# A transformer kernel on one core: GpSimd's second unit per layer norm in two halves, and the value products of the compressed stage in another order

## The chip, the core and the metric

The kernel runs on one core of one Trainium2 chip, as one program with one launch. The metric is the device time of that program in microseconds (us). The kernel before takes 1454.27 us, the median of three runs (1453.06 to 1454.77).

The engines have the profile's names: PE is TensorE (matrix products), ACT is ScalarE, DVE is VectorE, POOL is GpSimd, and SP issues most of the DMAs. Each runs its own list of instructions in the order in which the program was written, and they wait for each other through semaphores.

## The reference

Two transformer blocks over 256 tokens of width 1024, in fp32. The first block has a mixer with attention, a cross attention to a memory, and a SwiGLU, each with an RMS norm behind it. The second block has two layers. The part that matters here is the layer norm that closes each of its sublayers, and the shared keys and values that are taken from the state between the two layers:

```
def post_norm(x, sub, g, b):
    return layer_norm(DN_ALPHA * x + sub, g, b)
...
    for layer in range(DEPTH_2):
        if layer == N_A_LAYERS:
            shared = nsa_shared_kv(h, kv_w, cmp_pe, cmp_w1, cmp_b1, cmp_w2)
        h = post_norm(h, 0.5 * swiglu(h, ...), ln_g[layer, 0], ln_b[layer, 0])
        ...
        h = post_norm(h, mix, ln_g[layer, 1], ln_b[layer, 1])
        h = post_norm(h, 0.5 * swiglu(h, ...), ln_g[layer, 2], ln_b[layer, 2])
```

`kv = h @ kv_w` in `nsa_shared_kv` has six slots. Two of them, the values of the selected blocks and of the window, are the products "v2" and "v2w" below.

## The kernel before

**Tiles.** Tokens lie on the 128 partitions in two blocks, tb 0 and tb 1. A weight matrix is read in units of 128 x 2048 fp32 numbers (1 MB) through a ring of three slots. Every product is made in three passes of rounded fp32: ACT casts a unit to its high part `whi`, then DVE or POOL subtracts to get its low part `wlo`, and PE adds high times high, high times low and low times high. The state is split in the same way into `st_hi` (ACT) and `st_lo` (DVE), after PE has transposed it through PSUM. So each unit passes DMA, ACT, DVE or POOL, PE.

**Who makes the low parts.** DVE makes most of them (L2037). `BY_POOL` lists the units that POOL makes (`split`, L2797), among them the first two units behind each of five layer norms: "sgv", ("ffn", 2), "v2", "k2" and ("ffn", 4). ACT's `split` (L1453) casts a unit in one instruction.

**A layer norm.** The text names the norms by the state that they hand on: ln0 (in front of "sgv", at 608 us of the span), ln1 (in front of ffn 2, 753 us), ln2 (in front of "v2", 936 us), and ln4 (in front of ffn 4, 1258 us). A further norm closes the SwiGLU of layer 1's first sublayer (in front of "k2", 1150 us). For each token block DVE adds the branch to the state out of PSUM and takes statistics (`sum_out`, L2115 and L2121), makes mean and variance (L2107, L2108), then makes two passes that centre the halves of the row (`centre`, L2131) and two that scale them and add the offset (`scale`, L2144). These four passes are scalar_tensor_tensor instructions with two tensors from SBUF, and `gb` holds gain and offset. The two scale passes have no wait between them. The reciprocal root between them is POOL's (`var_root`, L2787). PE then transposes the two halves of the block (`turn_st`, L712), ACT copies them to `st_hi` (L1484), and DVE subtracts to get `st_lo` (`st_out`, L2059).

**POOL's order** around such a norm is `layer_norm(n, unit)`: split of the first unit, root of block 0, split of the second unit, root of block 1. ACT casts the second unit as soon as PE has let go of its slot in the ring.

**PE's order** behind a norm is `by_block`: both halves of block 0 are transposed (the first half already ahead of the end of the sublayer before), then come the products of block 0, for each unit and half of the row high times high (L766), weight's low part (L777), row's low part (L785). Behind the last high pass or the last low weight pass of block 0 it transposes the first half of block 1, and the second half a little later. For ln2 the "units" are "v2" and "v2w", of 256 columns each, so a pass of four matmuls is half as long there.

**DVE's order for ln2** differs from that of the other norms: the two `st_out` of block 0 stand between the sums of block 1, ahead of its variance. For ln0 only the first one does, and the second stands behind the variance.

Of the kernel before, what the change touches and what calls it, by code (L numbers as in the profile page):

```python
# [23 lines left out]
F32 = mybir.dt.float32  # L24
F32R = mybir.dt.float32r
I32 = mybir.dt.int32
ALU = mybir.AluOpType
# [3 lines left out]
P = 128  # L31
D = 1024
S = 256
KD = D // P
# [11 lines left out]
RING = 3  # L46
# [31 lines left out]
def build(nc, A, out):  # L78
    ctx = ExitStack()
    with ctx:  # L80
# [3 lines left out]
        def sem(name):  # L84
            return ctx.enter_context(nc.semaphore(name))


        raw = sb("raw", [P, RING, UNIT])
        minus_half = sb("minus_half", [P, 1])
        warm = sb("warm", [P, 16])  # L90
        whi = sb("whi", [P, RING, UNIT], F32R)
        wlo = sb("wlo", [P, RING, UNIT], F32R)
        st_hi = sb("st_hi", [P, 16, S], F32R)
        st_lo = sb("st_lo", [P, 16, S], F32R)
# [5 lines left out]
        res = sb("res", [P, 2, D])  # L100
# [69 lines left out]
        ws = carve(12288, 8, P)  # L170
# [7 lines left out]
        v2 = carve(9216, 2, 2, S)  # L178
# [40 lines left out]
        gain_ready = sem("gain_ready")  # L219
        half_hi_ready = sem("half_hi_ready")  # L220
        half_lo_ready = sem("half_lo_ready")
        whi_ready = sem("whi_ready")
        wlo_ready = sem("wlo_ready")
        w_used = sem("w_used")
        bank_full = [sem(f"bank_full{b}") for b in range(8)]
        bank_read = [sem(f"bank_read{b}") for b in range(8)]
        hi_rounded = sem("hi_rounded")
# [40 lines left out]
        unit_len = []  # L268
        first = {}
# [94 lines left out]
        split_no = {}  # L364
# [141 lines left out]
        def bank(key):  # L506
            return ps[:, use[key][0], :]
# [10 lines left out]
        def read(key, i=0):  # L518

            b, n = use[key]  # L520
            return bank_read[b], n + 1 + i
# [26 lines left out]
        for name in ("sgv", ("ffn", 2), "v2", "k2", ("ffn", 4)):  # L548
            BY_POOL |= {first[name], first[name] + 1}
        BY_POOL |= {first["ffn", n] + 3 for n in range(5)}  # L550

        def half_ready(name, tb, h):

# [108 lines left out]
        def _(pe):  # L662
# [176 lines left out]
            for h in range(2):  # L839
                pe.matmul(gain_rows(h), ones, gb[0:1, 1, 512 * h:512 * h + 512], start=True,  # L840
                          stop=True).then_inc(gain_ready, 1)
# [14 lines left out]
            u = first["kidx"]  # L856
# [340 lines left out]
            for n, j in enumerate(SGU_ORDER):  # L1197
# [7 lines left out]
                for m in MIX_AFTER.get(j, ()):  # L1205
# [4 lines left out]
            swiglu(2, "ln1", res, ahead=lambda: turn_st("ln2", res, 0, 0))  # L1210


            by_block([(first[name], KD, 256, 0, [bank(name)[:, tb * S:tb * S + S] for tb in range(2)], [name, name],
                       True, True) for name in ("v2", "v2w")], st="ln2", src=res)
            def cmp_in(slot):
                key = ("cin", slot)
                room(key)
# [220 lines left out]
        def _(act):  # L1438
# [9 lines left out]
            def split(u, s, q, n=UNIT):  # L1448
                act.wait_ge(raw_loaded[s], 32 * q if s < 2 else 32 * (q + 1))
                if not isinstance(u, int) or u >= RING:  # L1450

                    act.wait_ge(w_used, u - 2)
                act.copy(whi[:, s, 0:n], raw[:, s, 0:n]).then_inc(whi_ready, 1)  # L1453

            def upto(u):
                while nxt[0] <= min(u, UNITS - 1):
# [564 lines left out]
        def _(dve):  # L2021
# [29 lines left out]
            def st_out(name, tb, tiles=KD, k0=0, part=None):  # L2051

                for q in range(tiles // 4):
                    if part not in (None, q):
                        continue
                    key = ("st", name, tb, q)
                    dve.wait_ge(hi_rounded, split_no[key] + 1)
                    hi, lo = (x[:, k0 + 4 * q:k0 + 4 * q + 4, tb * P:tb * P + P] for x in (st_hi, st_lo))
                    dve.tensor_tensor(lo, bank(key).rearrange("p (k t) -> p k t", k=4), hi.bitcast(F32),  # L2059
                                      ALU.subtract).then_inc(*is_read(key))  # L2060
# [49 lines left out]
            def add_out(n, tb, h, halved):  # L2110

                f = 2.0 if halved else 1.0
                key = ("y", n, tb, h)
                dve.wait_ge(*full(key))
                dve.scalar_tensor_tensor(tmp[:, tb, 512 * h:512 * h + 512], res[:, tb, 512 * h:512 * h + 512], f * ALPHA,  # L2115
                                         bank(key), ALU.mult, ALU.add).then_inc(*is_read(key))

            def stats_out(n, tb, h):

                dve.wait_ge(*read(("y", n, tb, h)))  # L2120
                link(dve.bn_stats(stats[:, tb, 6 * h:6 * h + 6], tmp[:, tb, 512 * h:512 * h + 512]))  # L2121

            def sum_out(n, tb, h, halved):

                add_out(n, tb, h, halved)
                stats_out(n, tb, h)
# [7 lines left out]
            def norm_out(n, tb, between=None):  # L2134

                for r in range(2):
                    dve.wait_ge(gb_loaded[r], (GB0, GB1)[r][n])

                def centre(h):
                    link(centre_out(tb, h))  # L2140

                def scale(h):
                    t, r = (x[:, tb, 512 * h:512 * h + 512] for x in (tmp, res))
                    dve.scalar_tensor_tensor(r, t, root(n, tb), gb[:, 1, 512 * h:512 * h + 512], ALU.mult,  # L2144
                                             ALU.add).then_inc(res_ready, 1)

                if between is not None:
                    between()
                centre(0)
                if between is not None:  # L2150
                    scale(0)
                    centre(1)
                else:
                    centre(1)
                    scale(0)
                scale(1)

            def post_norm_ln(n, name, halved, early=False):

                eps = EPS2 * (4.0 if halved else 1.0)  # L2160
                if not early:
                    sum_out(n, 0, 0, halved)
                sum_out(n, 0, 1, halved)
                variance(n, 0, 2, eps)
                norm_out(n, 0)
                if name == "ln2":
                    add_out(n, 1, 0, halved)
                    st_out(name, 0, part=0)
                    stats_out(n, 1, 0)
                    st_out(name, 0, part=1)  # L2170
                    sum_out(n, 1, 1, halved)
                elif not early:
                    sum_out(n, 1, 0, halved)
                    if name is not None:
                        st_out(name, 0, part=0)
                    sum_out(n, 1, 1, halved)
                else:
                    sum_out(n, 1, 1, halved)
                    st_out(name, 0, part=0)
                variance(n, 1, 2, eps)  # L2180
                if name is None:
                    norm_out(n, 1)
                else:
                    norm_out(n, 1, between=lambda: st_out(name, 0, part=1) if name != "ln2" else None)
                if name is not None:
                    st_out(name, 1)

# [572 lines left out]
        def _(pool):  # L2760
            chain = [0]

            def link(ins):

                chain[0] += 1
                ins.then_inc(pool_step, 1)
                pool.wait_ge(pool_step, chain[0])
# [22 lines left out]
            def split(u):  # L2790

                s = u % RING
                pool.wait_ge(whi_ready, u + 1)

                pool.wait_ge(wlo_ready, u)
                n = unit_len[u]
                pool.tensor_tensor(wlo[:, s, 0:n], raw[:, s, 0:n], whi[:, s, 0:n].bitcast(F32),  # L2797
                                   ALU.subtract).then_inc(wlo_ready, 1)

            def norm_done(n):  # L2800
# [215 lines left out]
```

## Time and profile before

| what | value |
|---|---|
| median of three runs | 1454.27 us (1453.06 to 1454.77) |
| the profiled execution's own time | 1453.84 us |
| its span in the profile | 1452.1 us |
| PE busy | 1436.5 us, 99% of the span |
| DVE, ACT, POOL busy | 1075.3, 678.2, 206.9 us |
| PE's share of the chain that ended last | 91% |
| granted PE clock, mean | 0.998 of full speed |

All are of one core. The profile's span leaves out 1.7 us around the first and the last instruction. Busy times of matmuls are modelled where they overlap, so gaps of PE are read from the distance between starts in the timeline, and not from its busy share.

### The profile page before, as it was taken

What the parts mean: (1) busy time and instruction counts of PE and PEld (TensorE: products, weight loads), DVE (VectorE), ACT (ScalarE), POOL (GpSimd) and SP (SyncE); (2) the same over time, 40 slices, a digit from 0 to 9 for tenths busy, and PEclk for the clock granted to TensorE, in tenths of its full rate; (3) what the DMA queues carried; (4) which work ended last, traced back from release to release, by engine and by line L of the source; (5) the groups of instructions that cost most, each with busy time, mean ns of one, the idle gap of its engine ahead of it and who ended that gap; (6) DMA issues with size and microseconds to landing.
All of it is one profiled execution on the core that took longest, in us unless ns stands there. A gap on an engine that the chain in (4) does not pass through costs nothing.

```text
span 1452.1 us, 20728 instructions
## 1 busy us (share of the span) xinstructions
PE 1436.5 (99%) x7434; PEld 1210.7 (83%) x7434; DVE 1075.3 (74%) x1802; ACT 678.2 (47%) x848; POOL 206.9 (14%) x191
## 2 busy tenths in 40 slices
PE   9999999999999999999999999999999999999997
PEld 7988897888888888889988888888888897788886
DVE  4666766888778887767658887757877777688876
ACT  5346456544444344443434444435444378454342
POOL 1073011200001000300032000201000326510001
PEclk9999999999999999999999999999999999999999
DMA  8753563855656556565477655775556450465561
GB/s 254 254 174 121 195 222 99 303 192 175 209 193 204 188 173 206 171 231 176 168 237 241 201 173 191 243 232 174 173 192 212 146 179 31 145 232 173 186 214 63
DMA packets 198701, 273.94 MB, mean 189 GB/s; under 512 B 9585, under 2 KB 158193, under 8 KB 198386
## 3 DMA queue, kind: packets, MB, share of 16 engines
q1 hardware_dynamic: 194130, 256.10, 53.7%
q0 software_dynamic: 4368, 16.78, 3.2%
q8 instruction: 39, 0.64, 0.2%
q10 hardware_dynamic: 144, 0.26, 0.0%
q14 instruction: 20, 0.16, 0.0%
HBM read 271.80 MB, written 1.31 MB: 188 GB/s over the span
## 4 chain that ended last, share of the span: by engine, by line
PE 91%; POOL 3%; ACT 2%; DVE 2%; issue 1%; DVEq 0%; POOLq 0%; ACTq 0%
PE ps L671 26%; PE ps L672 26%; PE ps L673 26%; PE ps L785 3%; PE ps L766 3%; PE ps L777 3%; PE ps L712 1%; POOL wlo L2797 1%; ACT whi L1453 1%; PE ps L1191 0%; ACT big L1927 0%; PE ps L1227 0%; PE ps L1292 0%; POOL big L2843 0%; DVE big L2624 0%
## 5 line engine op out<-in xcount | busy, mean ns | idle before, releaser
L2037 DVE TENSOR_TENSOR wlo<-raw,whi 128x2048 fp32r<-128x2048 f32 (+1 forms) x221 | 502.2, 2290 | 167.9 <-ACT whi L1453 166.1
L1453 ACT CAST whi<-raw 128x2048 fp32r<-128x2048 f32 (+1 forms) x236 | 447.1, 1894 | 377.8 <-PE ps L673 329.8
L671 PE MATMUL ps<-whi,st_hi 128*128 128x512 f32 x1048 | 410.5, 392 | 0.0
L673 PE MATMUL ps<-whi,st_lo 128*128 128x512 f32 x1048 | 408.1, 389 | 0.0
L672 PE MATMUL ps<-wlo,st_hi 128*128 128x512 f32 x1048 | 407.9, 389 | 0.0
L2451 DVE STREAM_TRANSPOSE hidT<-hidden 32x128 f32<-32x128 f32 x800 | 242.3, 303 | 12.3
L673 PEld LDWEIGHTS ps<-whi,st_lo 128*128 128x128 f32 x1048 | 196.7, 188 | 41.0
L671 PEld LDWEIGHTS ps<-whi,st_hi 128*128 128x128 f32 x1048 | 196.8, 188 | 40.6 <-issue 0.3
L672 PEld LDWEIGHTS ps<-wlo,st_hi 128*128 128x128 f32 x1048 | 196.8, 188 | 40.1
L671 PE MATMUL ps<-whi,hid_hi 128*128 128x512 f32 x400 | 156.1, 390 | 0.0
L673 PE MATMUL ps<-whi,hid_lo 128*128 128x512 f32 x400 | 155.7, 389 | 0.0
L672 PE MATMUL ps<-wlo,hid_hi 128*128 128x512 f32 x400 | 155.7, 389 | 0.0
L2797 POOL TENSOR_TENSOR wlo<-raw,whi 128x2048 fp32r<-128x2048 f32 x15 | 69.5, 4631 | 573.0 <-ACT whi L1453 573.0
L671 PE MATMUL ps<-st_hi,whi 128*128 128x256 f32 (+1 forms) x464 | 133.1, 287 | 0.0
L672 PE MATMUL ps<-st_lo,whi 128*128 128x256 f32 (+1 forms) x464 | 131.2, 283 | 0.0
L673 PE MATMUL ps<-st_hi,wlo 128*128 128x256 f32 (+1 forms) x464 | 131.2, 283 | 0.0
L1729 ACT ACTIVATE silu<-ps 128x256 f32<-128x256 f32 x110 | 42.2, 384 | 153.6 <-PE ps L673 150.2
L2440 DVE TENSOR_TENSOR hidden<-ps,silu 128x256 f32<-128x256 f32 x110 | 45.9, 420 | 73.3 <-ACT silu L1729 73.3
L671 PEld LDWEIGHTS ps<-st_hi,whi 128*128 128x128 f32 (+1 forms) x464 | 88.4, 190 | 1.4 <-issue 1.2
L672 PEld LDWEIGHTS ps<-st_lo,whi 128*128 128x128 f32 (+1 forms) x464 | 88.4, 191 | 0.6 <-issue 0.5
L673 PEld LDWEIGHTS ps<-st_hi,wlo 128*128 128x128 f32 (+1 forms) x464 | 88.4, 190 | 0.0
L673 PEld LDWEIGHTS ps<-whi,hid_lo 128*128 128x128 f32 x400 | 75.1, 188 | 15.6
(262 smaller groups left out, 1421.8 us busy)
## 6 DMA issues: line engine op xcount, KB each, us to landing
raw<-in_ffn_w SPq DMA_DIRECT2D x264, 512.0 KB, 4.8
raw<-in_w_gate_up SPq DMA_DIRECT2D x44, 512.0 KB, 4.9
raw<-in_w_in SPq DMA_DIRECT2D x32, 512.0 KB, 4.8
raw<-in_sgu_w_in SPq DMA_DIRECT2D x32, 512.0 KB, 4.6
raw<-in_w_down SPq DMA_DIRECT2D x22, 512.0 KB, 5.1
raw<-in_sgu_w_out SPq DMA_DIRECT2D x16, 512.0 KB, 4.7
raw<-in_kv_w SPq DMA_DIRECT2D x12, 512.0 KB, 4.4
raw<-in_w_proj_attn SPq DMA_DIRECT2D x8, 512.0 KB, 4.4
```

Of the source, the lines that this page charges most:

```text
L671: pe.matmul(o, a[0], b[0], start=start, stop=False)
L672: pe.matmul(o, a[0], b[1], start=False, stop=False)
L673: return pe.matmul(o, a[1], b[0], start=False, stop=stop)
L766: pe.matmul(outs[tb], st_hi[:, k0 + k, t], w_hi[:, k, :], start=start and k == 0, stop=False)
L777: pe.matmul(outs[tb], st_hi[:, k0 + k, t], w_lo[:, k, :], start=False, stop=False)
L785: mm = pe.matmul(outs[tb], st_lo[:, k0 + k, t], w_hi[:, k, :], start=False, stop=stop and k == kt - 1)
L1453: act.copy(whi[:, s, 0:n], raw[:, s, 0:n]).then_inc(whi_ready, 1)
L1729: act.activation(silu[:, tb, :], bank(("up", n, tb))[:, 0:FC], ACT.Silu).then_inc(silu_ready, 1)
L2037: dve.tensor_tensor(wlo[:, s, 0:n], raw[:, s, 0:n], whi[:, s, 0:n].bitcast(F32), ALU.subtract).then_inc(wlo_ready, 1)
L2440: dve.tensor_tensor(hidden[:, tb, :], bank(("up", n, tb))[:, FC:2 * FC], silu[:, tb, :], ALU.mult).then_inc(*is_read(("up", n, tb)))
L2451: mm = dve.transpose(dst, src)
L2797: pool.tensor_tensor(wlo[:, s, 0:n], raw[:, s, 0:n], whi[:, s, 0:n].bitcast(F32), ALU.subtract).then_inc(wlo_ready, 1)
```

## The change

It has three parts.

1. The second unit of four of the norms (ln0, ln1, ln2, ln4; `IN_TWO`) is cast by ACT in two instructions of half a unit, the first of which signals `front_hi_ready`. POOL subtracts the front half when that has come, waits for its own instruction to end, then subtracts the back half. `wlo_ready` is signalled behind the back half.
2. DVE's order for ln2 becomes that of the other norms: the second `st_out` of block 0 moves from ahead of block 1's second sum to behind its variance.
3. The products "v2" and "v2w" get an order written out by hand (`both_values`). For block 0 the low row pass of the second half of "v2" moves behind the high passes of "v2w". Ten passes still stand between the transposes of block 0 and the first one of block 1.

```
-            by_block([(first[name], KD, 256, 0, ...) for name in ("v2", "v2w")], st="ln2", src=res)
+            def both_values():
...
+                turn_st("ln2", res, 0, 1)
+                for name in names:
+                    room(name)
+                high(0, 0, 0)
+                weight_low(0, 0, 0)
+                row_low(0, 0, 0)
+                high(0, 0, 1)
+                weight_low(0, 0, 1)
+                high(1, 0, 0)
+                high(1, 0, 1)
+                row_low(0, 0, 1)
+                weight_low(1, 0, 0)
+                row_low(1, 0, 0)
+                turn_st("ln2", res, 1, 0)
+                weight_low(1, 0, 1)
+                row_low(1, 0, 1)
...
@@ ScalarE, split
-                act.copy(whi[:, s, 0:n], raw[:, s, 0:n]).then_inc(whi_ready, 1)
+                front = n // 2 if isinstance(u, int) and u in IN_TWO else 0
+                if front:
+                    act.copy(whi[:, s, 0:front], raw[:, s, 0:front]).then_inc(front_hi_ready, 1)
+                act.copy(whi[:, s, front:n], raw[:, s, front:n]).then_inc(whi_ready, 1)
@@ VectorE, post_norm_ln
-                if name == "ln2":
-                    add_out(n, 1, 0, halved)
-                    st_out(name, 0, part=0)
-                    stats_out(n, 1, 0)
-                    st_out(name, 0, part=1)
-                    sum_out(n, 1, 1, halved)
-                elif not early:
+                if not early:
...
-                    norm_out(n, 1, between=lambda: st_out(name, 0, part=1) if name != "ln2" else None)
+                    norm_out(n, 1, between=lambda: st_out(name, 0, part=1))
@@ GpSimd, split
+                n = unit_len[u]
+                front = n // 2 if u in IN_TWO else 0
+                pool.wait_ge(wlo_ready, u)
+                if front:
+                    pool.wait_ge(front_hi_ready, IN_TWO[u])
+                    link(pool.tensor_tensor(wlo[:, s, 0:front], raw[:, s, 0:front], whi[:, s, 0:front].bitcast(F32),
+                                            ALU.subtract))
                 pool.wait_ge(whi_ready, u + 1)
-                pool.tensor_tensor(wlo[:, s, 0:n], raw[:, s, 0:n], whi[:, s, 0:n].bitcast(F32),
+                pool.tensor_tensor(wlo[:, s, front:n], raw[:, s, front:n], whi[:, s, front:n].bitcast(F32),
                                    ALU.subtract).then_inc(wlo_ready, 1)
```

## Rows read from the trace of the kernel before

**Rows 1.** The page: busy us of each engine, share of the span, instructions.

```profile
PE 1436.5 (99%) x7434; PEld 1210.7 (83%) x7434; DVE 1075.3 (74%) x1802; ACT 678.2 (47%) x848; POOL 206.9 (14%) x191
```

**Rows 2.** Timeline, TensorE, ln0: start us, duration us, engine, line, work, count, [idle, releaser].

```profile
612.04 0.60 PE L712 MATMUL ps<-con,res 128*128 128x128 f32 x4
...
615.23 1.07 PE L766 MATMUL ps<-whi,st_hi 128*128 128x512 f32 x4
616.14 1.07 PE L777 MATMUL ps<-wlo,st_hi 128*128 128x512 f32 x4
617.63 0.66 PE L712 MATMUL ps<-con,res 128*128 128x128 f32 x4 [0.42 <-DVE res L2144]
```

**Rows 3.** Timeline of TensorE, ln1.

```profile
757.56 0.60 PE L712 MATMUL ps<-con,res 128*128 128x128 f32 x4
...
761.90 1.07 PE L777 MATMUL ps<-wlo,st_hi 128*128 128x512 f32 x4
763.11 0.65 PE L712 MATMUL ps<-con,res 128*128 128x128 f32 x4
```

**Rows 4.** Timeline of TensorE, ln2.

```profile
940.15 0.60 PE L712 MATMUL ps<-con,res 128*128 128x128 f32 x4
...
944.97 0.64 PE L766 MATMUL ps<-whi,st_hi 128*128 128x256 f32 x4
946.11 0.63 PE L712 MATMUL ps<-con,res 128*128 128x128 f32 x4 [0.50 <-issue]
```

**Rows 5.** Timeline of GpSimd, ln0.

```profile
611.11 4.63 POOL L2797 TENSOR_TENSOR wlo<-raw,whi 128x2048 fp32r<-128x2048 f32 x1 [1.73 <-ACT whi L1453]
```

**Rows 6.** Timeline of VectorE, ln0.

```profile
609.77 1.42 DVE L2144 SCALAR_TENSOR_TENSOR res<-tmp,rstd,gb 128x512 f32<-128x512 f32 x2
...
616.82 0.75 DVE L2144 SCALAR_TENSOR_TENSOR res<-tmp,rstd,gb 128x512 f32<-128x512 f32 x1 [0.53 <-POOL rstd L2787]
```

**Rows 7.** Timeline of ScalarE, ln0.

```profile
609.12 1.91 ACT L1453 CAST whi<-raw 128x2048 fp32r<-128x2048 f32 x1 [3.65 <-PE ps L673]
```

**Rows 8.** Line 1476 by itself: durations in ns, min/median/max.

```profile
L1476 ACT CAST whi<-raw x2: 1048/1060/1071, 242.1 to 246.3; 128x1024 fp32r<-128x1024 f32 x2
```

**Rows 9.** Timeline of VectorE, ln1.

```profile
755.21 1.42 DVE L2144 SCALAR_TENSOR_TENSOR res<-tmp,rstd,gb 128x512 f32<-128x512 f32 x2
```

**Rows 10.** Timeline of VectorE, ln2.

```profile
937.90 1.42 DVE L2144 SCALAR_TENSOR_TENSOR res<-tmp,rstd,gb 128x512 f32<-128x512 f32 x2
...
940.27 0.69 DVE L2059 TENSOR_TENSOR st_lo<-ps,st_hi 128x512 fp32r<-128x512 f32 x1 [0.35 <-ACT st_hi L1484]
...
945.26 0.75 DVE L2144 SCALAR_TENSOR_TENSOR res<-tmp,rstd,gb 128x512 f32<-128x512 f32 x1 [0.53 <-POOL rstd L2787]
```

**Rows 11.** Timelines of GpSimd and VectorE, norm of layer 3, whole unit.

```profile
1153.06 4.63 POOL L2797 TENSOR_TENSOR wlo<-raw,whi 128x2048 fp32r<-128x2048 f32 x1 [1.72 <-ACT whi L1453]
...
1156.30 1.94 DVE L2131 SCALAR_TENSOR_TENSOR tmp<-tmp,mv,gb 128x512 f32<-128x512 f32 x1
```

**Rows 12.** Timelines of GpSimd and VectorE, norm ahead of ffn0, half a unit.

```profile
246.51 2.41 POOL L2885 TENSOR_TENSOR wlo<-raw,whi 128x1024 fp32r<-128x1024 f32 x1
...
247.81 1.66 DVE L2096 SCALAR_TENSOR_TENSOR res<-tmp,rstd,res 128x512 f32<-128x512 f32 x1
```

**Rows 13.** Timelines of GpSimd and VectorE, pooling stage.

```profile
87.55 0.74 POOL L2838 TENSOR_TENSOR big<-big 128x257 f32<-128x257 f32 x1
...
86.80 0.88 DVE L2258 TENSOR_SCALAR big<-big 128x384 f32<-128x384 f32 x1
87.61 2.83 DVE L2037 TENSOR_TENSOR wlo<-raw,whi 128x2048 fp32r<-128x2048 f32 x1
...
111.74 2.29 DVE L2037 TENSOR_TENSOR wlo<-raw,whi 128x2048 fp32r<-128x2048 f32 x1 [0.45 <-ACT whi L1453]
```

**Rows 14.** Timelines of GpSimd and VectorE, last norm.

```profile
1441.37 1.00 POOL L2787 TENSOR_TENSOR rstd<-meansq,minus_half 128x1 f32<-128x1 f32 x1 [160.24 <-DVE meansq L2108]
...
1441.21 1.40 DVE L2131 SCALAR_TENSOR_TENSOR tmp<-tmp,mv,gb 128x512 f32<-128x512 f32 x2
```

More of the change, by code:

```diff
@@ L221, in build @@
         half_lo_ready = sem("half_lo_ready")
+        front_hi_ready = sem("front_hi_ready")
         whi_ready = sem("whi_ready")
@@ L550, in build @@
         BY_POOL |= {first["ffn", n] + 3 for n in range(5)}
+        IN_TWO = {first[name] + 1: i + 1 for i, name in enumerate(("sgv", ("ffn", 2), "v2", ("ffn", 4)))}
         def half_ready(name, tb, h):
@@ L1210, in _, with high, weight_low, row_low @@
             swiglu(2, "ln1", res, ahead=lambda: turn_st("ln2", res, 0, 0))
-            by_block([(first[name], KD, 256, 0, [bank(name)[:, tb * S:tb * S + S] for tb in range(2)], [name, name],
-                       True, True) for name in ("v2", "v2w")], st="ln2", src=res)
+            def both_values():
+                names = ("v2", "v2w")
+                ws = [[w[:, first[name] % RING, :].rearrange("p (k c) -> p k c", k=KD) for w in (whi, wlo)]
+                      for name in names]
+                def high(n, tb, q):
+                    pe.wait_ge(whi_ready, first[names[n]] + 1)
+                    pe.wait_ge(hi_rounded, split_no["st", "ln2", tb, q] + 1)
+                    part(n, tb, q, st_hi, 0)
+                def weight_low(n, tb, q):
+                    pe.wait_ge(wlo_ready, first[names[n]] + 1)
+                    part(n, tb, q, st_hi, 1)
+                def row_low(n, tb, q):
+                    pe.wait_ge(*read(("st", "ln2", tb, q)))
+                    return part(n, tb, q, st_lo, 0)
+                def part(n, tb, q, x, w):
+                    for k in range(4 * q, 4 * q + 4):
+                        mm = pe.matmul(bank(names[n])[:, tb * S:tb * S + S], x[:, k, tb * P:tb * P + P],
+                                       ws[n][w][:, k, :], start=(x is st_hi and w == 0 and k == 0),
+                                       stop=(x is st_lo and k == KD - 1))
+                    return mm
+                turn_st("ln2", res, 0, 1)
[14 more added lines that the diff above has]
+                row_low(1, 0, 1)
+                for n in range(2):
+                    high(n, 1, 0)
+                    if n == 0:
+                        turn_st("ln2", res, 1, 1)
+                    weight_low(n, 1, 0)
+                    row_low(n, 1, 0)
+                    high(n, 1, 1)
+                    weight_low(n, 1, 1)
+                    row_low(n, 1, 1).then_inc(w_used, 1)
@@ L1215, in cmp_in @@
+            both_values()
             def cmp_in(slot):
@@ L2792, in split @@
                 s = u % RING
+                n = unit_len[u]
[5 more added lines that the diff above has]
+                                            ALU.subtract))
                 pool.wait_ge(whi_ready, u + 1)
-                pool.wait_ge(wlo_ready, u)
-                n = unit_len[u]
-                pool.tensor_tensor(wlo[:, s, 0:n], raw[:, s, 0:n], whi[:, s, 0:n].bitcast(F32),
+                pool.tensor_tensor(wlo[:, s, front:n], raw[:, s, front:n], whi[:, s, front:n].bitcast(F32),
                                    ALU.subtract).then_inc(wlo_ready, 1)
```

## The prediction

> **What bounds the kernel now.** I read the page first: TensorE is busy for 1436.5 us, 99% of the span [rows 1], so an edit gains only what it takes out of TensorE's gaps, and loses whatever it adds to them. Then I read TensorE's timeline behind each of the four norms that the change touches, from start to start. In ln0 a group of four matmuls of 512 columns takes 0.91 (615.23 to 616.14), so the group of 616.14 is through at 617.05, and the next transposes begin at 617.63: a gap of 0.58, ended by VectorE's new state [rows 2]. In ln1 the same sum gives 762.81 against 763.11, a gap of 0.30 [rows 3]; ln4 repeats ln1 within 0.05. In ln2 a group has 256 columns and takes about half of 0.91, so it is through at about 945.45, and the transposes begin at 946.11: 0.66 [rows 4]. The four gaps are 1.86 us together. That is all that the change can win, 0.13% of the time.
>
> What ends these gaps is VectorE's first scale pass of block 1, and in front of it VectorE itself had been idle for 0.53 in ln0 [rows 6] and for 0.53 in ln2 [rows 10], waiting for GpSimd's root, which stands behind GpSimd's split of the second unit: 4.63 from 611.11 on in ln0 [rows 5]. So the change aims at the right wait. The question is what lies beside the earlier start.
>
> **Part 1, the split in halves: when the front half starts.** ScalarE's cast begins at 609.12 and takes 1.91 [rows 7]; GpSimd began 0.08 behind its end [rows 5]. A cast of half a unit takes 1.05 to 1.07 [rows 8]. So GpSimd's front half will start at 609.12 + 1.05 + 0.08 = 610.25 instead of 611.11. ScalarE pays 2 x 1.05 - 1.91 = 0.2 more, and GpSimd, with 2.41 for half a unit [rows 12], 2 x 2.41 - 4.63 = 0.2 plus one wait for itself; ScalarE's 0.2 lies in its idle time (without that cover, 0.8 us for four norms at most).
>
> **What it starts into.** VectorE's two scale passes of block 0 run from 609.77 to 611.19; each is 0.75 long, so the second begins at 610.44 [rows 6]. Before, GpSimd began as the second one ended. Now its front half falls into the first one, 0.19 ahead of the second. In ln1 the passes begin at 755.21 and 755.88 [rows 9]; by the same sum the front half starts at 755.76, 0.12 ahead of the second. In ln2 they begin at 937.90 and 938.57 [rows 10], the front half at 938.36, 0.21 ahead; in ln4 it is 0.19.
>
> **What such an overlap costs** is shown four times in other places of this trace. At the norm of layer 3 a whole split holds GpSimd from 1153.06 to 1157.69; a centre pass that VectorE begins at 1156.30 takes 1.94 instead of 0.75 and ends at 1158.24, 0.55 behind GpSimd [rows 11]. A half split to 248.92 stretches another pass of the same kind, begun at 247.81, to 1.66; it ends 0.55 behind GpSimd too [rows 12]. So a pass with two tensors from SBUF stands still until GpSimd's subtraction is through. Who goes first when GpSimd arrives in the middle of one pass with another right behind it is shown in the pooling stage: GpSimd's 87.55 falls into VectorE's pass of 86.80 to 87.68; the next VectorE instruction starts at 87.61, 0.06 later than GpSimd, and takes 2.83 where a free one takes 2.29, ending 2.15 behind GpSimd's end [rows 13]. GpSimd had gone ahead of it. The last norm agrees: GpSimd's root begins at 1441.37 inside the first of two passes that have no wait between them, and is done at 1442.37, before the pair is (1442.61) [rows 14]: it went in between.
>
> The Trainium skill speaks against this change in the same way: "SBUF — State Buffer", section "Who interferes with whom", says that VectorE's second read interface is GpSimd's too, held as a lock for a whole instruction, so that a VectorE instruction with two SBUF inputs and a GpSimd instruction that reads SBUF exclude each other, and that the order of issue decides who blocks. By that rule the time is that of the forecast below; without it, that of rival A. The 1.94 and the 1.66 above agree with it.
>
> **The sum in ln0.** The first scale pass ends at 610.52. GpSimd's front half then goes ahead: 2.41 less what it had spent waiting (0.1 to 0.2), so it ends at about 612.8. The second scale pass ends 0.55 later, 613.35 instead of 611.19: VectorE is 2.16 late. Behind it in VectorE's list stand all of block 1's sums, its variance, and the state's low parts. TensorE's transposes of block 0's second half can begin at 613.4 instead of 612.04 [rows 2]: TensorE stands 1.4 at once. Block 1's scale pass comes at 616.82 - 0.53 + 2.16 = 618.45 (GpSimd's back half, behind the late scale pass, is through at about 615.7, so the root no longer makes it wait), and the transposes at 617.63 - 0.53 + 2.16 = 619.26. TensorE would be there at 617.05 + 1.4 = 618.45. Loss: 619.26 - 617.63 = 1.6.
>
> **ln1 and ln4.** The first scale pass of ln1 ends at 755.96, the front half at 758.25, the second pass at 758.8 instead of 756.63. The transposes that stood at 757.56 [rows 3] begin at 758.87, 1.3 late. VectorE had been waiting for TensorE's last sums there, so it loses only about 1.0 and is no longer last: block 1's transposes begin when TensorE gets there, at 762.81 + 1.3 = 764.1, or 764.0 without 0.13 that it now spends waiting in that stretch. Against 763.11 the loss is 0.9. ln4 the same: 0.9.
>
> **Parts 2 and 3, ln2.** The reorder on VectorE moves one subtraction of 0.69 behind the variance and drops a wait of 0.35 for ScalarE; the number of its instructions stays. The new order on TensorE has the same 24 groups, ten of them between the transposes, and costs nothing by itself; it asks for the moved low part two groups later. With the port free, the root would be early enough and the scale pass of block 1 could come 0.35 + 0.53 sooner than 945.26 [rows 10], which covers the gap of 0.66. With the collision the second scale pass of block 0 ends at 938.65 + 2.3 + 0.55 = 941.5 instead of 939.32. From there to block 1's scale pass VectorE took 945.26 - 939.32 = 5.94, of which 0.53 + 0.35 were waits, so 5.06 of work: the scale pass runs from 946.55 to 947.3, and the transposes begin at 947.4 instead of 946.11 [rows 4]. TensorE comes to it 1.4 late (941.55 against 940.15) less its old gap, so VectorE is last. Loss: 1.3. Behind ln2 SyncE's loads wait for the norm's last pass, and move with TensorE.
>
> Sum: 1.6 + 0.9 + 0.9 + 1.3 = 4.7 us. The profiled execution would go from 1453.84 to 1458.5. It stands 0.43 below the median of 1454.27, so the median goes to 1459.0. Bounds: 0.6 to 2.0 for each norm (the lead is smallest in ln1; ends of passes are read to 0.1), 2.6 to 6.2 in all.
>
> **Rivals.**
> A. *The halves do what they are for.* GpSimd's front half runs beside VectorE's second scale pass without holding it. Then all four gaps close as far as VectorE's idle time allows: 0.53 + 0.30 + 0.32 + 0.6 = 1.8 faster, 1452.5. For it: other VectorE passes (one tensor from PSUM, one from SBUF) overlap GpSimd's split unharmed (0.69, [rows 10]). Against it: [rows 11 to 13]. It decides where the second pass gets its operands ahead of GpSimd and GpSimd is not delayed in turn.
> B. *VectorE keeps the port through both passes.* GpSimd then starts reading only at 611.19 in ln0, as before, and the two halves end 0.2 later than the whole did: 0.2 lost in each of ln0, ln1 and ln4, 0.6 won in ln2 by the reorder. 1454.3, no change. For it: the leads of 0.12 to 0.21 are short, and a cast 0.2 longer than in [rows 8] turns it. Against it: [rows 13, 14], where 0.06 was enough.
>
> **How the numbers follow.** Forecast 0.67, A 0.15, B 0.17, something else, slower, 0.01. A measurement of this kernel tells about 0.2%, 2.9 us, from no change: faster is below 1451.4, slower above 1457.2. Of the forecast 0.62 lies above 1457.2 and 0.05 (fewer norms collide) below; of A 0.02 is faster; B is all within. Faster 0.02, same 0.35, slower 0.63. The likeliest case's own range is 1456.9 to 1460.5. To hold 8 in 10 the range has to reach through B to A's time: 1452.5 to 1460.5.
>
> **What would show it.** If I am right, in the changed profile the second L2144 pass of block 0 is some 2.9 long in the four norms, right behind a GpSimd instruction of half a unit, the second set of TensorE's transposes starts 1.3 to 1.4 behind the first free moment, and GpSimd's root is no longer waited for. If that pass stays at 0.75 and TensorE's gap ahead of block 1's transposes is gone, A holds; if it stays at 0.75 and GpSimd's front half is 3 long, B. I am wrong in size if only some of the four collide.

## The result and the profile after

The changed kernel takes 1461.09 us, the median of six runs (1459.06 to 1461.72), beside 1454.38 (1453.06 to 1454.77) of the kernel before: a ratio of 1.0046 [1.0036, 1.0056], slower by 0.46%. The direction was forecast; the time is 2.1 us above the forecast and 0.6 above the end of its range. The profiled execution took 1461.41, with a span of 1459.7 us, 7.6 longer than before. For the profiled execution the forecast was 1458.5, 2.9 lower. TensorE's work is the same and its busy time grew by only 1.2 [rows 1], so most of the 7.6 is gaps:

```profile
PE 1437.7 (98%) x7434; PEld 1211.9 (83%) x7434; DVE 1084.1 (74%) x1802; ACT 678.9 (47%) x852; POOL 207.6 (14%) x195
```

I measured each norm by itself, from the start of its first transposes to the start of block 1's first transposes, which is where the next gap ended before. In the rows below these are the L714 groups of four matmuls (L712 in the kernel before). The table gives that distance and, in brackets, what it lost against before; all are in us, read from TensorE's timeline.

| kernel | ln0 | ln1 | ln2 | ln4 | lost in all |
|---|---|---|---|---|---|
| before | 6.72 | 6.92 | 7.09 | 6.93 | |
| changed | 8.38 (1.66) | 7.69 (0.77) | 11.52 (4.43) | 7.76 (0.83) | 7.69 |
| forecast | (1.6) | (0.9) | (1.3) | (0.9) | 4.7 |

The four stages hold the whole difference (7.69 against 7.6 of span). Three norms came as forecast; ln2 lost three times as much as it should have.

**ln0, as forecast.** The timelines of GpSimd, VectorE and TensorE of the changed kernel (start us, duration us, engine, line, work, count, [idle before, releaser]):

```profile
610.41 2.48 POOL L2849 TENSOR_TENSOR wlo<-raw,whi 128x1024 fp32r<-128x1024 f32 x1 [0.92 <-ACT whi L1509]
612.96 2.73 POOL L2852 TENSOR_TENSOR wlo<-raw,whi 128x1024 fp32r<-128x1024 f32 x1
617.32 0.56 POOL L2838 TENSOR_TENSOR rstd<-meansq,minus_half 128x1 f32<-128x1 f32 x1 [1.63 <-DVE meansq L2165]
...
609.89 3.54 DVE L2201 SCALAR_TENSOR_TENSOR res<-tmp,rstd,gb 128x512 f32<-128x512 f32 x2
613.36 0.68 DVE L2172 SCALAR_TENSOR_TENSOR tmp<-res,ps 128x512 f32<-128x512 f32 x1
618.59 0.75 DVE L2201 SCALAR_TENSOR_TENSOR res<-tmp,rstd,gb 128x512 f32<-128x512 f32 x1
...
611.01 0.60 PE L714 MATMUL ps<-con,res 128*128 128x128 f32 x4
...
613.49 0.66 PE L714 MATMUL ps<-con,res 128*128 128x128 f32 x4 [1.18 <-DVE res L2201]
...
619.39 0.66 PE L714 MATMUL ps<-con,res 128*128 128x128 f32 x4 [0.69 <-DVE res L2201]
```

The pair of scale passes that took 1.42 [rows 6] takes 3.54. Its first pass is 0.75 long; the second begins at 610.56 and is 2.87 long, ending at 613.43, 0.54 behind GpSimd's front half (610.41 + 2.48 = 612.89). GpSimd had come 0.15 ahead of the second pass. TensorE's second transposes stand 1.18 for it. The root, which was waited for in [rows 6], is now early: the scale pass at 618.59 has no idle time ahead of it, but it comes 1.77 later than before.

**ln2, not as forecast.** TensorE's timelines: the first transposes of the kernel before, then the changed kernel:

```profile
939.02 0.60 PE L712 MATMUL ps<-con,res 128*128 128x128 f32 x4
...
941.52 0.60 PE L714 MATMUL ps<-con,res 128*128 128x128 f32 x4
...
944.00 0.66 PE L714 MATMUL ps<-con,res 128*128 128x128 f32 x4 [1.18 <-DVE res L2201]
946.69 0.71 PE L1236 MATMUL ps<-whi,st_hi 128*128 128x256 f32 x4 [2.03 <-issue]
947.25 0.64 PE L1236 MATMUL ps<-wlo,st_hi 128*128 128x256 f32 x4
947.72 0.85 PE L1236 MATMUL ps<-whi,st_lo 128*128 128x256 f32 x4
948.37 1.05 PE L1236 MATMUL ps<-whi,st_hi 128*128 128x256 f32 x4
949.22 1.05 PE L1236 MATMUL ps<-wlo,st_hi 128*128 128x256 f32 x4
950.07 1.70 PE L1236 MATMUL ps<-whi,st_hi 128*128 128x256 f32 x8
951.62 0.64 PE L1236 MATMUL ps<-whi,st_lo 128*128 128x256 f32 x4
952.09 0.64 PE L1236 MATMUL ps<-wlo,st_hi 128*128 128x256 f32 x4
952.56 0.64 PE L1236 MATMUL ps<-whi,st_lo 128*128 128x256 f32 x4
953.04 0.60 PE L714 MATMUL ps<-con,res 128*128 128x128 f32 x4
```

The hole of 1.18 ahead of 944.00 is the one of ln0 again. Two things stand behind it that the forecast does not have. First, a second hole of 2.03 between the transposes and the first product; before, the product came 0.36 behind the transposes (940.15 [rows 4] to 940.51). The profile puts it down to "issue", so it names no releaser. Second, the groups of four at 948.37 and 949.22 are 0.85 apart, where undisturbed ones are 0.47 to 0.48 apart (951.62, 952.09, 952.56). The windows of the same stretch (us, its length, busy us of PE, PEld, DVE, ACT and POOL with counts, granted clock of TensorE, DMA share, GB/s) say why:

```profile
947.00:948.00 1.00, 1.00 (x11) 1.00 (x10) 0.93 (x4) 0.08 (x1) 0.17 (x1) 0.98 0.00 0
948.00:949.00 1.00, 1.00 (x7) 1.00 (x6) 1.00 (x2) 0.00 (x0) 0.39 (x1) 0.50 0.00 0
949.00:950.00 1.00, 1.00 (x6) 1.00 (x6) 0.96 (x3) 0.00 (x0) 0.00 (x0) 0.50 0.00 0
950.00:951.00 1.00, 1.00 (x7) 1.00 (x6) 0.96 (x2) 0.00 (x0) 0.00 (x0) 0.50 0.00 0
951.00:952.00 1.00, 1.00 (x9) 1.00 (x9) 0.30 (x1) 0.00 (x0) 0.41 (x1) 0.81 0.00 0
```

The granted clock is at 0.50, the 1.2 GHz level, for 3.4 us; it fell 1.3 us behind the second hole. The ten groups between the transposes take 6.35 (946.69 to 953.04) where e5_order below does them in 4.88. So the 4.43 of ln2 are 1.35 (second transposes late), 2.33 (first product 2.69 behind them instead of 0.36) and 1.47 (clock), less 0.72 for the old gap ahead of block 1's transposes, which is gone (0.66 in the prediction, and 0.06 by which the ten groups were slower before than in e5_order).

### The profile page after: what moved, and what is told of

It is laid out like the page before. It is cut to its first block, busy times and chain, and to the rows that moved or that the text cites. A ratio compares the mean times of both kernels' runs of the same rounds, so it can differ in the third digit from the quotient of the medians.

```text
span 1459.7 us, 20741 instructions
## 1 busy us (share of the span) xinstructions
PE 1437.7 (98%) x7434; PEld 1211.9 (83%) x7434; DVE 1084.1 (74%) x1802; ACT 678.9 (47%) x852; POOL 207.6 (14%) x195
## 4 chain that ended last, share of the span: by engine, by line
PE 90%; DVE 5%; ACT 2%; POOL 2%; issue 1%; DVEq 0%; POOLq 0%
PE ps L673 25%; PE ps L675 25%; PE ps L674 25%; PE ps L768 3%; PE ps L787 3%; PE ps L779 3%; PE ps L714 1%; DVE res L2201 1%; PE ps L1236 1%; DVE tmp L2188 1%; PE ps L1193 0%; ACT big L1984 0%; PE ps L1281 0%; DVE stats L2178 0%; DVE tmp L2172 0%
## 5 line engine op out<-in xcount | busy, mean ns | idle before, releaser
L2852 POOL TENSOR_TENSOR wlo<-raw,whi 128x2048 fp32r<-128x2048 f32 (+1 forms) x15 | 61.9, 4124 | 572.1 <-ACT whi L1510 571.8
```

The costliest lines, as they stand in the source:

```text
L2852: pool.tensor_tensor(wlo[:, s, front:n], raw[:, s, front:n], whi[:, s, front:n].bitcast(F32), ALU.subtract).then_inc(wlo_ready, 1)
```

## The experiments

**Theories.** One: GpSimd's front half holds VectorE's second scale pass in all four norms, and in ln2 the hand-written order adds a wait for a PSUM bank. `both_values` asks for the banks of "v2" and "v2w" together, ahead of the first product; `by_block` asked for v2w's only ahead of its own first pass. The bank is freed by VectorE's last sum of block 1, the second L2172 pass behind the scale passes. (A bank is the part of PSUM that a product is summed in; `room` is TensorE's wait until the bank's last reader is done.) Rival: the halves cost by themselves (more instructions and waits on three engines), and the new order of the passes is what stops TensorE in ln2. All edits but two are made to the changed kernel.

**e1_room**: v2w's bank is asked for ahead of its own first pass.

```
-                for name in names:
-                    room(name)
+                room(names[0])
                 high(0, 0, 0)
...
                 weight_low(0, 0, 1)
+                room(names[1])
                 high(1, 0, 0)
```

> The changed kernel with one edit: TensorE waits for the bank of v2w right ahead of the first v2w pass instead of ahead of the first v2 pass. If the up-front wait for v2w's bank is what made ln2 cost 4.4 us (it holds TensorE until VectorE has added the last quarter of block 1), ln2's stretch between the two first transposes falls from 11.5 to about 8.4, the granted clock stays at 1.00 there, and the time is 1458.0. If the collision on VectorE's pass alone starves TensorE and takes the clock down, ln2 stays above 10 us with the clock at 0.5 for some 3 us, and the time is 1460 or more.

Measured: 1458.34 us (1455.84 to 1459.56, 10 runs), ratio to before 1.0032 [1.0022, 1.0041]. ln0, ln1 and ln4 lose 1.64, 0.77 and 0.82 as in the changed kernel; ln2 loses 1.37 instead of 4.43. TensorE's timeline in ln2:

```profile
943.89 0.66 PE L714 MATMUL ps<-con,res 128*128 128x128 f32 x4 [1.18 <-DVE res L2201]
944.49 0.73 PE L1236 MATMUL ps<-whi,st_hi 128*128 128x256 f32 x4
...
945.95 0.74 PE L1236 MATMUL ps<-whi,st_lo 128*128 128x256 f32 x4 [0.25 <-DVE st_lo L2116]
...
949.88 0.60 PE L714 MATMUL ps<-con,res 128*128 128x128 f32 x4
```

The second hole is gone with two lines moved, and with it the fall of the clock, which stays at 1.00 through the stage. What is left in ln2 is 1.37, where the forecast had 1.3; the way to it is not quite the forecast's (see the section on the prediction).

**e2_whole**: no halves; the early demand for both banks stays (`IN_TWO = {}`).

> The changed kernel without part 1: the second units are cast and split whole, the new orders of ln2 stay. If the collision comes from the early front half, VectorE's second scale pass of block 0 is 0.75 long again in all four norms, and ln0, ln1 and ln4 have the lengths of the kernel before. If the up-front bank wait counts, ln2 still has a hole of about 1.5 us ahead of its first pass: 1455.2 with the clock staying up, 1456.9 if a hole of that length takes it down. If the bank wait costs nothing, ln2 gains its old gap: 1453.8.

Measured: 1453.65 us (1452.37 to 1455.25, 11 runs), ratio 1.0004 [0.9995, 1.0013]. No scale pass is longer than 0.75 in any norm. ln2 loses 0.81, the other three 0.05 to 0.07 each. TensorE and VectorE in ln2:

```profile
940.38 0.60 PE L714 MATMUL ps<-con,res 128*128 128x128 f32 x4
942.28 0.71 PE L1236 MATMUL ps<-whi,st_hi 128*128 128x256 f32 x4 [1.30 <-issue]
...
941.50 0.68 DVE L2172 SCALAR_TENSOR_TENSOR tmp<-res,ps 128x512 f32<-128x512 f32 x1
```

VectorE's last sum ends at 941.50 + 0.68 = 942.18 and TensorE starts 0.10 later. In the changed kernel the same sum runs from 945.92 to 946.60 and TensorE starts at 946.69, 0.09 later. That is the releaser that the profile does not name. The hole costs less here than it is long, since the old gap ahead of block 1's transposes takes 0.7 of it.

**e7_room_first**: the kernel before, with nothing changed but the place of the demand.

```
+            turn_st("ln2", res, 0, 1)
+            for name in ("v2", "v2w"):
+                room(name)
             by_block([(first[name], KD, 256, 0, ...) for name in ("v2", "v2w")], st="ln2", src=res)
```

> The kernel before with one edit: TensorE waits for both banks of v2 and v2w ahead of the first pass of ln2. No halves, old order on VectorE, so no collision. The bank wait theory: TensorE stands about 2.4 us until VectorE's last sum is read (942.9 in the trace of before), then 10 passes: 1.8 us lost, 1456.2, and about 1457.9 if a hole of 2.4 us with no collision takes the clock to half for 3.4 us as in the changed kernel. If only the collision makes the loss: 1454.4.

Measured: 1455.75 us (1453.27 to 1457.03, 11 runs), ratio 1.0013 [1.0004, 1.0022]. ln2 loses 1.74, the other norms at most 0.02. TensorE and VectorE in ln2:

```profile
938.72 0.60 PE L712 MATMUL ps<-con,res 128*128 128x128 f32 x4
941.55 0.71 PE L766 MATMUL ps<-whi,st_hi 128*128 128x256 f32 x4 [2.23 <-issue]
...
940.77 0.68 DVE L2118 SCALAR_TENSOR_TENSOR tmp<-res,ps 128x512 f32<-128x512 f32 x1
```

Again 0.10 from the end of VectorE's last sum (941.45) to the product. So it is the place of the demand that makes the wait, not the order of the passes. This hole of 2.23 stands alone, and the clock stays at 1.00 behind it.

**e3_halves**: the kernel before with part 1 alone, the old order of ln2 on VectorE and TensorE.

> The kernel before with part 1 alone: halves, but the old orders of VectorE and TensorE in ln2. The collision theory: second scale pass of 2.9 us in all four norms, ln0 +1.7, ln1 and ln4 +0.8 each, ln2 +1.3 (the forecast's own sum), clock at 1.00: 1459.0. If the bank wait of part 3 is not what made ln2 dear, ln2 loses about 4 here too: 1461.

Measured: 1458.9 us (1456.72 to 1459.13, 5 runs), ratio 1.0037 [1.0023, 1.0051]. All four second scale passes take 2.87; the norms lose 1.64, 0.75, 1.68 and 0.82. ln2 lost 0.3 to 0.4 more than expected. e1_room, which has the same halves and the new order, loses 1.37 there, so the new order is worth 0.3 when the bank does not stop it; e5_order finds the same 0.3 without halves.

**e8_ln2**: halves ahead of "v2" alone, with the early demand (`IN_TWO = {first["v2"] + 1: 1}`).

> The changed kernel with halves ahead of v2 alone (the new order and the early demand for the bank stay). ln0, ln1 and ln4 as in the kernel before. In ln2 both holes of TensorE follow one another: 1.2 for the collision and 2.0 for the bank. If these two together bring the granted clock down, as in the profile of the changed kernel, it is at 0.5 for some 3.4 us again and block 1's transposes stand at about +11.5: 4.4 lost, 1458.4. The rival, that the fall in the changed kernel was of that one execution or came from the earlier norms' holes: the clock stays up, block 1's transposes stand at about +9.8 (1.35 + 2.0 - 0.66 = 2.7 lost), 1456.7.

Measured: 1458.72 us (1458.61 to 1459.15, 5 runs), ratio 1.0041 [1.0027, 1.0054]. The other norms lose 0.07 each, ln2 4.41. TensorE in ln2, and the windows behind it:

```profile
941.68 0.66 PE L714 MATMUL ps<-con,res 128*128 128x128 f32 x4 [1.17 <-DVE res L2201]
944.37 0.71 PE L1236 MATMUL ps<-whi,st_hi 128*128 128x256 f32 x4 [2.04 <-issue]
...
950.71 0.60 PE L714 MATMUL ps<-con,res 128*128 128x128 f32 x4
```

```profile
944.00:945.00 1.00, 0.63 (x5) 0.66 (x6) 0.97 (x2) 0.76 (x1) 0.00 (x0) 1.00 0.00 0
946.00:947.00 1.00, 1.00 (x7) 1.00 (x6) 0.96 (x3) 0.00 (x0) 0.07 (x1) 0.50 0.00 0
```

The fall of the clock came back with the two holes, in another kernel and with no holes in the earlier norms. It is not an accident of one execution. Of the single holes (1.18 in e1_room, 1.30 in e2_whole, 2.23 in e7_room_first) none brought it, each in the one execution that was profiled. Whether one hole as long as the two together (3.2) would bring it too was not tried.

**e4_late**: e1_room's edit, and GpSimd's front half waits for VectorE's second scale pass. `BEHIND` names the norm in front of the unit.

```
                 if front:
+                    pool.wait_ge(res_ready, RES[BEHIND[u]] + 2)
                     pool.wait_ge(front_hi_ready, IN_TWO[u])
```

> The changed kernel with the bank of v2w asked for just ahead of its first pass (as in e1_room), and GpSimd's front half waits until VectorE's second scale pass of block 0 is done. It keeps the two casts and the two subtractions. If the port is what costs (the forecast's mechanism): the second scale pass is 0.75 again in all four norms, the second transposes are no longer late (+1.1 to +1.4 behind the first instead of +2.5 to +2.7), GpSimd's two halves end about 0.3 to 0.5 later than the whole unit did before, so block 1's transposes stand at about +6.9 to +7.2 in ln0, ln1 and ln4 and +7.0 in ln2: about 1455.0, bounds 1454 to 1456. The rival, that two halves cost by themselves (more casts, more waits), gives the same lateness as e1_room: +8.4 in ln0, 1458.3.

Measured: 1455.76 us (1453.1 to 1456.14, 11 runs), ratio 1.001 [1.0001, 1.0019]. The norms lose 0.51, 0.45, 0.17 and 0.51. VectorE and GpSimd in ln0:

```profile
609.78 1.42 DVE L2203 SCALAR_TENSOR_TENSOR res<-tmp,rstd,gb 128x512 f32<-128x512 f32 x2
617.34 0.75 DVE L2203 SCALAR_TENSOR_TENSOR res<-tmp,rstd,gb 128x512 f32<-128x512 f32 x1 [0.53 <-POOL rstd L2840]
...
611.37 2.40 POOL L2852 TENSOR_TENSOR wlo<-raw,whi 128x1024 fp32r<-128x1024 f32 x1 [1.99 <-DVE res L2203]
613.85 2.42 POOL L2855 TENSOR_TENSOR wlo<-raw,whi 128x1024 fp32r<-128x1024 f32 x1
```

With the same casts and the same two subtractions, but no overlap with the scale passes, the pair of scale passes is back at 1.42 and the second transposes are in time in all four norms (+1.13, +1.36, +1.13, +1.36). The rest of the loss is a later root: GpSimd starts 0.26 later than before and needs 0.27 more for two halves (611.37 to 616.27 against 4.63), so the root ends 0.5 later and is waited for again. (The back half still meets a centre pass of block 1, which takes 1.24 at 615.57 instead of 0.75; it costs nothing here, since VectorE then waits 0.53 for the root.) The stages stand at 7.23, 7.37, 7.26 and 7.44, up to 0.3 above what was expected; the rival's 8.4 in ln0 is out.

**e6_quarter**: e1_room with a front part of a quarter (`front = n // 4`).

> As e1_room, but the front part is a quarter of the unit instead of a half: a dose of the same collision. If VectorE's second scale pass stands still until GpSimd's instruction is through, its length follows GpSimd's: a quarter is about 1.3, the front starts about 0.5 earlier, so the pass is 1.0 to 1.9 instead of 2.87, and the second transposes stand at about +1.5 to +1.9 in ln0; block 1's at about +6.9 to +7.4 in ln0, ln1 and ln4 no more than 0.2 from before: about 1454.7. If the hold had nothing to do with the length of GpSimd's instruction, the pass takes 2.87 again and the time is that of e1_room, 1458.3.

Measured: 1454.42 us (1452.15 to 1455.31, 11 runs), ratio 1.0002 [0.9992, 1.0011]. ln0 loses 0.57, ln2 0.29; ln1 and ln4 gain 0.19 and 0.13. VectorE and GpSimd in ln0:

```profile
609.77 2.45 DVE L2201 SCALAR_TENSOR_TENSOR res<-tmp,rstd,gb 128x512 f32<-128x512 f32 x2
...
609.87 1.81 POOL L2849 TENSOR_TENSOR wlo<-raw,whi 128x512 fp32r<-128x512 f32 x1 [0.49 <-ACT whi L1509]
```

The second scale pass takes 1.78 instead of 2.87 and ends at 612.22, 0.54 behind GpSimd's 611.68: the same distance as with the half. The hold follows GpSimd's instruction. The quarter came at 609.87, inside the first scale pass (609.77 to 610.52), and took 1.81, longer than a quarter needs (an estimate: half of the 2.40 in e4_late, 1.2): by that estimate GpSimd waited some 0.6 itself, until that pass was done at 610.5, and then went ahead of the second.

**e5_order**: e1_room with no halves (`IN_TWO = {}`): parts 2 and 3 alone, with the bank asked for late.

> Parts 2 and 3 alone with the bank of v2w asked for just ahead of its first pass: no halves. If the wait for the bank was all that the new order of the value products cost, block 1's transposes of ln2 stand at +6.4 to +6.6 (before +7.09, with the wait for the bank in e2_whole +7.90), ln0, ln1 and ln4 as before: 1453.4, about 0.6 below the kernel before. The rival, that the order itself costs (the moved low part comes late, or other waits), gives +7.1 or more in ln2 and 1454.0 or more.

Measured: 1454.07 us (1452.33 to 1454.8, 11 runs), ratio 1.0004 [0.9995, 1.0013]. ln2 stands at 6.80, a gain of 0.29, between the two expectations. TensorE's first and tenth group, then GpSimd and VectorE in ln2:

```profile
940.65 0.72 PE L1236 MATMUL ps<-whi,st_hi 128*128 128x256 f32 x4
...
945.05 0.64 PE L1236 MATMUL ps<-whi,st_lo 128*128 128x256 f32 x4
...
939.43 4.64 POOL L2852 TENSOR_TENSOR wlo<-raw,whi 128x2048 fp32r<-128x2048 f32 x1 [1.77 <-ACT whi L1510]
...
945.16 0.75 DVE L2201 SCALAR_TENSOR_TENSOR res<-tmp,rstd,gb 128x512 f32<-128x512 f32 x1 [0.53 <-POOL rstd L2838]
```

With 0.48 for the tenth group the ten take 4.88 (940.65 to 945.53). The wait of 0.35 for ScalarE [rows 10] is gone, but the root behind GpSimd's whole unit is still waited for, with the same 0.53. My expectation of 0.6 forgot this: without the halves the order can win little. The order itself costs nothing, as the prediction had it; its demand for the bank does.

**e9_two**: what the stages left as gain, put together: e6_quarter with `IN_TWO` for ln1 and ln4 alone.

> What the runs so far leave as gain, put together: the new order of ln2 with v2w's bank asked for late (e5_order: -0.3 in ln2), and a front part of a quarter in ln1 and ln4 alone (e6_quarter: -0.2 and -0.1 there). If the stages add up: block 1's transposes at +6.72 in ln0, +6.73 in ln1, +6.80 in ln2 and +6.80 in ln4, 0.6 below the kernel before, 1453.3: less than these rounds can tell from no change. The rival, that the quarter's late state in ln1 and ln4 is given back behind the norm, gives 1454.0 or more.

Measured: 1451.52 us (1450.36 to 1453.9, 11 runs) beside 1453.89, ratio 0.9994 [0.9985, 1.0003]: no change that these runs can tell. The stages stand at 6.79, 6.74, 6.78 and 6.80, 0.55 better than before together, as expected. The two medians are 2.4 apart, more than the stages show; spans that differ by some 2 us without an edit stand in the last section. It is no worse than the kernel before and not shown to be better.

All losses side by side, from the same distances as in the first table:

| kernel | ln0 | ln1 | ln2 | ln4 | in all | ratio to before |
|---|---|---|---|---|---|---|
| changed | 1.66 | 0.77 | 4.43 | 0.83 | 7.69 | 1.0046 [1.0036, 1.0056] |
| e1_room | 1.64 | 0.77 | 1.37 | 0.82 | 4.60 | 1.0032 [1.0022, 1.0041] |
| e3_halves | 1.64 | 0.75 | 1.68 | 0.82 | 4.89 | 1.0037 [1.0023, 1.0051] |
| e8_ln2 | 0.07 | 0.07 | 4.41 | 0.07 | 4.62 | 1.0041 [1.0027, 1.0054] |
| e7_room_first | 0.02 | 0.00 | 1.74 | -0.01 | 1.75 | 1.0013 [1.0004, 1.0022] |
| e4_late | 0.51 | 0.45 | 0.17 | 0.51 | 1.64 | 1.0010 [1.0001, 1.0019] |
| e2_whole | 0.05 | 0.07 | 0.81 | 0.06 | 0.99 | 1.0004 [0.9995, 1.0013] |
| e6_quarter | 0.57 | -0.19 | 0.29 | -0.13 | 0.54 | 1.0002 [0.9992, 1.0011] |
| e5_order | 0.06 | 0.07 | -0.29 | 0.06 | -0.10 | 1.0004 [0.9995, 1.0013] |
| e9_two | 0.07 | -0.18 | -0.31 | -0.13 | -0.55 | 0.9994 [0.9985, 1.0003] |

Norms that keep the whole unit lose 0.05 to 0.07 in the kernels built on the changed one and nothing in e7_room_first. GpSimd's split of ln0 starts at 611.17 in e5_order and at 611.11 before [rows 5], behind a cast that begins at 609.12 in both. The changed code waits for the slot of the low part first and for the cast second, the other way round than before; that this is the cause was not tried.

## Why the prediction was right and where it failed

**Right: the collision.** The front half was forecast to start at 610.25 in ln0, 0.19 ahead of the second scale pass; it started at 610.41, 0.15 ahead, in a stage that began 0.10 later. In ln1 the lead was 0.06 (757.62 to 757.68), half of the forecast's 0.12, and the pass was held all the same. The pass was forecast at some 2.9 and took 2.87 in all four norms. That GpSimd goes between two passes that follow each other without a wait was read from [rows 13, 14], and the 0.55 between GpSimd's end and the pass's end from [rows 11, 12]; both hold, though [rows 14] shows little by itself: the pair of passes there takes 1.40, no longer than the undisturbed 1.42 of [rows 6]. e4_late shows the cause: with the overlap with the scale passes taken away and the halves kept, the loss of all four norms falls from 4.60 (e1_room) to 1.64. The rule of the Trainium skill that the prediction cited ("SBUF — State Buffer", section "Who interferes with whom") agrees with the 2.87 here and with the 0.75 of the same pass in e4_late.

**Right: the sums of ln0, ln1 and ln4.** 1.6, 0.9 and 0.9 were forecast; 1.66, 0.77 and 0.83 came.

**Right in ln2, with some luck: the collision's term.** It was forecast at 1.3 with the new order, and e1_room, which has just that, lost 1.37. VectorE's part came as forecast: its scale pass of block 1 stands 7.56 behind the first transposes (948.98 less 941.42) where the forecast had 7.53. But the forecast had TensorE there well ahead of it, 1.4 late less the old gap of 0.66. TensorE was as late as VectorE: the first product came 0.24 later behind the second transposes than before (0.60 instead of 0.36), and the ten groups took 5.39 instead of 4.88, 0.25 of it a wait for the state's low part. The transposes at 949.88 have no idle time ahead of them. The two paths happened to end together.

**Not right in ln2: what the old wait was for.** The prediction put the 0.53 ahead of VectorE's scale pass down to a root that stands behind GpSimd's split. In ln0 it does. In ln2 of the kernel before, the split was through at 943.85 and GpSimd then waited for VectorE's variance:

```profile
944.12 1.02 POOL L2787 TENSOR_TENSOR rstd<-meansq,minus_half 128x1 f32<-128x1 f32 x1 [0.27 <-DVE meansq L2108]
```

So the halves alone had nothing to win there: in e3_halves GpSimd is idle for 2.10 ahead of that root, and VectorE's scale pass still waits 0.53 for it.

**Failed: "the new order on TensorE has the same 24 groups ... and costs nothing by itself".** I counted the passes and did not count the waits. The diff moves one: `room("v2w")` from ahead of v2w's first pass to ahead of v2's. It takes effect only because the bank is still being read: v2w's bank holds a quarter of the sublayer's result (block 1, second half of the row), which VectorE adds to the state in the last of its four sums, 2.6 behind the second transposes in the changed kernel. In e7_room_first this one move loses 1.74 in a kernel that has nothing else changed. The prediction named what is queued behind VectorE's late pass, but did not do the same for TensorE's list.

**Failed: the bounds.** "0.6 to 2.0 for each norm" had no term for the clock. With the second hole right behind the first, the granted clock falls to the 1.2 GHz level, and the ten groups take 1.47 longer. The losses do not add: the early demand alone loses 0.81 (e2_whole), the halves alone in the new order 1.37 (e1_room), both together 4.43. Of the 2.25 between, 1.47 is the clock and 0.79 the bank's hole, which is 2.33 with the halves and 1.54 without: VectorE is later than TensorE by that much, since its stand behind GpSimd is longer than the stand that it causes. (Two smaller terms cancel: the 0.75 that TensorE lost behind the transposes in e1_room, and the old gap of 0.72, which each of the two kernels takes off for itself.)

**Rivals.** A (the halves win 1.8) and B (VectorE keeps the port, 1454.3) both fell on the 2.87. Halves that do not overlap, which is what B describes, were tried as e4_late: B had 0.2 lost in each of ln0, ln1 and ln4 and 0.6 won in ln2; what came is 0.45 to 0.51 lost in each of the three and 0.17 lost in ln2. Some 0.26 of each norm is the later start of GpSimd there, behind a semaphore of VectorE, which B does not have.

## What to carry to other kernels

When an order of products is rewritten by hand, list the semaphore waits that move, with what each PSUM bank last held and who reads it last: the passes may cost the same while one early wait stops them all. Before GpSimd's work is moved earlier, look at which VectorE passes with two SBUF operands it will land on; it goes between two of them, and the second then lasts until GpSimd's whole instruction is done, so the size of that instruction is the price. And where two gaps of TensorE come close together, do not price them at their sum: here the granted clock fell to 0.50 behind them, in both kernels that had them.

## What the hardware showed that was not expected

**The clock.** Holes of 1.18 and 2.03 us with one group of transposes between them brought the granted clock to 0.50 for 3.4 us, in the changed kernel and in e8_ln2, 1.0 to 1.3 us behind the end of the second hole. A single hole of 2.23 did not in the one execution of e7_room_first that was profiled, which does not say that it never does: behind a program's last product the clock fell 2.1 us after TensorE stopped in the kernel before, 4.2 in the changed kernel and 5.3 in e2_whole. With the fall in them, ten groups of four matmuls of 256 columns took 6.35 instead of 4.88. Holes are not all that goes with a fall: e3_halves has one near its start, from 8.5 to 11.9, and TensorE had been busy from 1.64 to 9.43 without a hole (its mean from 8 to 12 us is 0.57, in the rows at the end of this section). What brought that one stays open.

**GpSimd waits too.** A quarter of a unit that arrived inside a VectorE pass took 1.81 instead of about 1.2, so the hold goes both ways: who has begun finishes first. The kernel before shows it without an estimate. In the stage of [rows 13], GpSimd's next instruction falls into VectorE's pass of 87.61 to 90.44 and lasts until 90.51; the same instruction takes 0.22 four us later:

```profile
88.36 2.15 POOL L2841 TENSOR_TENSOR big<-big,con 128x16 f32<-128x16 f32 x1
...
92.32 0.22 POOL L2841 TENSOR_TENSOR big<-big,con 128x16 f32<-128x16 f32 x1
```

The back half in the changed kernel, which met the end of the late scale pass, took 2.73 instead of the 2.42 of e4_late.

**The start of the program.** TensorE does its first products at different speeds in different executions. The windows of TensorE near the start, of the kernel before and of e3_halves (us, length, busy us and matmuls, granted clock, DMA share, GB/s):

```profile
4.00:8.00 4.00, 4.00 (x9) 1.00 0.91 282
```

```profile
4.00:8.00 4.00, 4.00 (x17) 1.00 0.93 279
8.00:12.00 4.00, 3.69 (x14) 0.57 1.05 397
```

From 4 to 8 us TensorE is busy throughout in both, but does 9 matmuls in the one and 17 in the other; four matmuls that begin at 4.92 in both take 3.78 and 2.04. The column of the clock reads 1.00 there in both, so these rows do not show what makes the difference. ln0 then begins at 610.91 and at 608.87. That execution of e3_halves took 1456.72, 2.2 below the median of its kernel. Spans can so differ by 2 us for no cause in an edit, and stages were compared from their own starts.
